# Other banks for the layer projections at two norms of the first block, and another place for one norm's spread

## The reference

```python
def first_block(x, ...):                                   # one layer
    z = rmsnorm(h, norm_mix_pre) @ w_in                    # pool input, q, k, v, gates
    y_pool = pool_mixer(p) @ w_branch_pool
    y_attn = moba_attention(q, k, v) @ w_branch_attn
    m = sigmoid(g_pool) * y_pool + sigmoid(g_attn) * y_attn
    h = h + rmsnorm(m @ w_out, norm_mix_post)              # joint 1: norm, residual, next norm
    u2 = rmsnorm(h, norm_mlp_pre)
    a = square(relu(u2 @ w_up))                            # 1024 -> 4096
    h = h + rmsnorm(a @ w_down, norm_mlp_post)             # joint 2: the same
def second_block(x, p, ...):                               # two layers: diff. attention, windowed attention
    hn = rms_norm(h, attn_norm[i]); h = h + mixer(hn)
    h = h + conv_ffn(rms_norm(h, ffn_norm[i]))
    gate = sigmoid(rms_norm(h, ple_norm[i]) @ ple_w_gate[i])
    h = h + (p[i] @ ple_w_proj[i]) * gate                  # p @ ple_w_proj depends on no h
    return rms_norm(h, final_norm)
```

## Time and profile before

| | |
|---|---|
| median of 3 runs | 1990.87 us (1989.4 to 1992.05) |
| profiled execution | 1990.34 us, its span 1988.6 us |
| mean granted TensorE clock | 0.994 of full speed |
| TensorE busy | 1951.0 us (98%) |
| VectorE, ScalarE, GpSimd busy | 1195.8, 924.6, 1113.9 us |
| joint 1 (columns to the next product) | 319.78 to 333.28 us |
| joint 2 | 688.47 to 701.28 us |

### The profile page before, as it was taken

How to read it: one execution, slowest core, us unless ns; L and a number is a source line. 1 busy time by engine, 2 the same in 40 slices (tenths; PEclk the granted TensorE clock), 3 DMA queues, 4 the chain that set the end, 5 groups by cost and what they waited for, 6 DMA issues and landing times.

```text
span 1988.6 us, 25389 instructions
## 1 busy us (share of the span) xinstructions
PE 1951.0 (98%) x9308; PEld 1602.0 (81%) x9308; DVE 1195.8 (60%) x2004; ACT 924.6 (46%) x1740; POOL 1113.9 (56%) x847
## 2 busy tenths in 40 slices
PE   8999999999999999999999999999999999999997
PEld 6877887888888877878788888888777888888886
DVE  6773324353433488877676646856688775745855
ACT  5653336433333356545353433445477543443443
POOL 5344545454444456454566665755784576666652
PEclk9999999999999999999999999999999999999998
DMA  4122233232232321111323222223110322222221
GB/s 159 64 70 95 96 106 128 85 111 101 96 113 91 122 82 64 53 59 59 128 95 105 96 97 95 96 89 109 64 54 33 128 96 105 96 85 98 103 96 53
DMA packets 52107, 182.73 MB, mean 92 GB/s; under 512 B 5776, under 2 KB 6160, under 8 KB 51984
## 3 DMA queue, kind: packets, MB, share of 16 engines
q1 hardware_dynamic: 51984, 181.12, 26.0%
HBM read 174.80 MB, written 6.29 MB: 91 GB/s over the span
## 4 chain that ended last, share of the span: by engine, by line
PE 95%; DVE 3%; ACT 1%; issue 0%; DMA 0%; POOL 0%; SPq 0%; DVEq 0%; POOLq 0%
PE b L394 29%; PE b L396 28%; PE b L395 28%; PE b L416 3%; PE b L408 2%; PE b L449 1%; PE b L459 1%; PE b L440 1%; PE b L409 1%; PE b L439 1%; PE b L410 1%; PE b L427 0%; PE b L429 0%; PE b L428 0%; DMA raw<-in_w_first 0%
## 5 line engine op out<-in xcount | busy, mean ns | idle before, releaser
L240 POOL TENSOR_TENSOR ra<-raw,ra 128x512 fp32r<-128x512 f32 x632 | 881.0, 1401 | 781.7 <-ACT ra L284 779.1
L394 PE MATMUL b<-ra 128*128 128x512 f32 x2528 | 1001.9, 396 | 20.3 <-POOL ra L240 9.6
L396 PE MATMUL b<-ra 128*128 128x512 f32 x2528 | 986.6, 390 | 0.0
L395 PE MATMUL b<-ra 128*128 128x512 f32 x2528 | 985.8, 390 | 0.0
L284 ACT ACTIVATE ra<-raw 128x512 fp32r<-128x512 f32 x632 | 392.6, 628 | 536.4 <-PE b L396 529.9
L394 PEld LDWEIGHTS b<-ra 128*128 128x128 f32 x2528 | 475.8, 188 | 126.6 <-issue 17.1
L396 PEld LDWEIGHTS b<-ra 128*128 128x128 f32 x2528 | 475.4, 188 | 101.2
L395 PEld LDWEIGHTS b<-ra 128*128 128x128 f32 x2528 | 476.1, 188 | 93.2
L732 DVE TENSOR_TENSOR h<-b,h 128x512 f32<-128x512 f32 x136 | 91.7, 683 | 60.3 <-PE b L396 59.6
L623 DVE TENSOR_TENSOR tmp<-b,rb 128x512 f32<-128x512 f32 x64 | 43.9, 690 | 126.2 <-PE b L396 126.1
L616 DVE TENSOR_TENSOR ra<-b,ra 128x512 fp32r<-128x512 f32 (+4 forms) x166 | 91.7, 567 | 18.1 <-ACT ra L335 15.4
(11 more groups left out here) (277 smaller groups left out, 1929.8 us busy)
## 6 DMA issues: line engine op xcount, KB each, us to landing
raw<-in_f_g SPq DMA_DIRECT2D x40, 512.0 KB, 3.5
raw<-in_f_v SPq DMA_DIRECT2D x40, 512.0 KB, 3.5
raw<-in_f_d SPq DMA_DIRECT2D x40, 512.0 KB, 3.4
raw<-in_w_up SPq DMA_DIRECT2D x32, 512.0 KB, 3.5
raw<-in_w_down SPq DMA_DIRECT2D x32, 512.0 KB, 3.5
raw<-in_p_g SPq DMA_DIRECT2D x16, 512.0 KB, 3.5
raw<-in_w_gp SPq DMA_DIRECT2D x8, 512.0 KB, 3.5
raw<-in_w_ga SPq DMA_DIRECT2D x8, 512.0 KB, 3.5
```

What stands on the lines that cost most here:

```text
L240: e.tensor_tensor(wl, src, wh.bitcast(F), ALU.subtract).then_inc(*w_low.mark(n))
L394: e.matmul(ps, wh[:, c:c + 128], xh, start=start, stop=False)
L395: e.matmul(ps, wh[:, c:c + 128], xl, start=False, stop=False)
L396: last = e.matmul(ps, wl[:, c:c + 128], xh, start=False, stop=stop)
```

## The change

`LATER` gets a fifth value, -0.4, for rank -6, and the spread of a norm with `keep` gets this rank: it may be placed up to 0.4 us before its inputs are estimated ready, where it was placed 0.6 us after. The banks of both joints are dealt anew. At joint 1 `LB7` stands as 5, 6, 0, 1, 2, 3, 4: `spare` is now 2 and 3, and the projection takes 0, 4, 1 in turn. At joint 2 `spare` is 4 and 5, and the projection takes 2, 6, 3 in turn.

```diff
-LATER = (1.5, 4.0, 0.6, 2.5)
+LATER = (1.5, 4.0, 0.6, 2.5, -0.4)
...
-        yield -4 if x["rank"] == -2 else -3, "pe", lambda: None if bank_free[STB] is None else (v, *bank_free[STB])
+        yield -6 if x["keep"] else -4 if x["rank"] == -2 else -3, "pe", lambda: None if bank_free[STB] is None else (
+            v, *bank_free[STB])
         x["spread"] = t = spread(0, v)
...
-        spare += LB7[4:]
-        yield from layer_projection(0, LB7[:4])
+
+
+        spare += LB7[4:6]
+        yield from layer_projection(0, [LB7[2], LB7[6], LB7[3]])
...
-                yn3, u3 = post_norm("mlp_post", ("attn", 0), now("pe"), [4, 5, 6])
+                yn3, u3 = post_norm("mlp_post", ("attn", 0), now("pe"), [4, 5])
...
-        yield from layer_projection(1, [0, 1, 2, 3])
+        yield from layer_projection(1, [2, 6, 3])
```

## The result

The changed kernel takes 1987.85 us (median of 20 runs, 1985.84 to 1989.36) against 1992.16 us of the kernel before in 20 runs beside it: ratio 0.9979, 95% interval 0.9973 to 0.9985, so 4.2 us less (3.0 to 5.4). On a second chip the median was 1986.23 against 1991.42 us: 0.9974 (0.9964 to 0.9985). The profiled execution took 1987.47 us, its span 1985.7, where 1990.34 and 1988.6 stood before: 2.9 us less.

A forecast was written before the change was run, and what follows sets the result against it. TensorE, busy 98% of the span, bounds the kernel; both joints wait for ScalarE's copy. Gains of 1.2 + 1.6 + 0.2 = 3.0 us take the median from 1990.87 to 1987.9 us, range 1985.0 to 1991.5.

The forecast's parts named there:

- joint 1: The step from the first block's attention to its MLP; 2.57 us of TensorE time lost there before the change.
- joint 2: The step from the MLP to the second block's attention; TensorE idle 2.40 us there before the change.
- The spread, 1.2 us sooner: At joint 1, the spread behind 12 matmuls after the columns instead of 18, starting about 324.5 instead of 325.70.
- Seven steps in 3.61 us: At joint 1, ScalarE's awaited copy still seven steps, 3.61 us, behind the new chunk's high part, so starting at 331.09.
- TensorE's start, 0.99 us behind the copy's: At joint 1, the next layer's first product starts 0.99 us after ScalarE's awaited copy starts, at 332.08: 1.20 us gained.
- The low clock behind joint 1, 1.6 us: The 1.2 GHz stretch after joint 1 stays away once the wait shrinks from 2.4 to 1.1 us: 1.6 us gained.
- The wait for line 702, 1.1 us: At joint 2, the first projection waits for VectorE's accumulation on bank 2: 1.1 us later, between 0.9 and 1.3.
- Joint 2's end, 0.2 us gained: The product ending joint 2 starts at 701.03 instead of 701.28; 0.2 us taken, between -0.3 and 0.6.
- A (the low clock stays): Rival: the low-clock stretch does not go, or returns at another wait; gain 1.4 us, 1989.5 us; chance 0.20.
- B (both waits vanish): Rival: ScalarE's queue does not decide, and both joints' waits vanish; gain 5.6 us, 1985.3 us; chance 0.13.
- Rival C: Bank 2's wait at joint 2 is not regained, lower clock there, joint 1 keeps its own; +1.5, 1992.4 us; chance 0.10.
- D (all shifts cancel): Rival: at both joints the spread or second projection waits, so the change does nothing; 1990.9 us; chance 0.07.

## Why the prediction was right, and where it was off

The forecast of 1987.9 us, by 1.2 + 1.6 + 0.2 = 3.0 us, came in at 1987.85 and inside its range; against the runs of before beside it the gain is 4.2 us. The profiled execution gave 2.9 us, of which the segments of the joints are 3.16 and the start 0.26 of loss. That the time itself came so close is in part luck: the forecast started from the median of three runs, 1990.87, and twenty runs of the same kernel gave 1992.16, 1.3 us more. The gain, 3.0 us by the forecast, is at the lower end of the measured interval (3.0 to 5.4).

- **Bank 4 at joint 1, 0.1 us.** Right: 318.67 to 318.99 is 0.32 us instead of 0.23.
- **The spread, 1.2 us sooner.** Right: less the 0.26 us by which joint 1 starts later it stands at 324.46; forecast "about 324.5". VectorE's root ended at 324.50 + 0.16 = 324.66, 0.06 us before it.
- **Seven steps in 3.61 us.** Right to the hundredth, and with it that "not needed next" does not shorten ScalarE's queue. The high part and the copy stand at 327.54 and 331.15, forecast 327.48 and 331.09.
- **TensorE's start, 0.99 us behind the copy's.** Wrong by 0.3 us: it is 0.69 (332.10 for 331.41), since fewer waits stand before the matmul. I had taken a distance of the trace for a constant; in it lie 0.36 us from the copy's end, of which 0.3 go with the waits, as the test with fewer waits shows. So joint 1 gained 1.44 us and not 1.20.
- **The low clock behind joint 1, 1.6 us.** Right in size: 3.06 - 1.44 = 1.62. The prediction called it "the least certain term" because joint 2 had no drop. In five executions with over 2 us of idle at joint 1 the stretch came five times, in the nine others never, the one with dummy matmuls among them. The Trainium skill (TensorE: Matmul & The Clock Gate, Terms) prices such a stretch at its length times the share withheld; the trace agrees, with 1.62 us for the prediction's estimate of 1.7.
- **The wait for line 702, 1.1 us.** Right: the start is at 683.21 where 682.27 was due (685.07 less the 2.80 us that all is sooner), 0.94, and the columns at 688.88 by the old count of time, forecast 688.89; the spread at 693.45, forecast 693.44.
- **Joint 2's end, 0.2 us gained.** Mis-sized at the place, near in the end: the product starts 0.45 us sooner (698.03 + 2.80 = 700.83 for 701.28), again by the shorter way from the copy to the matmul. The copy itself stood at 700.15 by the old count, 0.12 us later than forecast: the prediction took joint 1's 2.98 us from the spread to the first high part, where the rows of joint 2 give 2.80 before, and the new profile has 3.08. Of the 0.45 us, 0.3 is given back in the second block before the last line 427, in both profiles of the change. Nearly all of it goes at one place on TensorE:

```profile
826.91 0.63 PE L416 MATMUL b<-ident,fa 128*128 128x128 f32 x4 [0.19 <-DVE fa L581]
```

The matmuls ahead of this one start 3.14 us sooner than before, this one 2.89. The wait stands in both profiles of the change (0.19 and 0.17 us) and at this place in none of before or of the version with bank 3 first, whose segment keeps its gain. What makes VectorE late there is not shown.
- **What the forecast did not contain.** The kernel before pays the low stretch at joint 2 too, in some executions: over all versions, in one of six with an idle of 1.87 us or more there. The change's idles of 0.78 and 0.75 us had none in two. A pair of profiles need not show this part of the gain in the median. It fits that joint 1 alone was timed at -2.4 and the whole change at -4.2 and -5.2, with joint 2's segment worth only 0.1; but these intervals overlap, and one execution is no rate. How much of the 4.2 us it makes stays open.

Of the rivals, A (the low clock stays) fell with the window behind joint 1. B (both waits vanish) fell for the change, but is nearly what the banks alone do: my objection, that ScalarE's queue decides, held only for the order that the sooner spread makes. Rival C had the wait of bank 2 right and what follows from it wrong: joint 2 got its time back, no lower clock came there, and joint 1's went. The awaited copy at joint 2 stood at 697.35, which is 700.15 by the old count, before the 700.9 from which it decides. The Trainium skill's rule that small idle pieces on cycling banks bring the lower clock (TensorE: Matmul & The Clock Gate, A second HAM failure mode: psum-queue depth-cycling), on which C leaned, did not show: two idles, of 0.78 and 0.75 us within 15 us, left the clock at 1.00. D (all shifts cancel) fell with the spread and the new order of the banks, which moved as forecast.

The deeper miss is in the reading of the change, not in its sum. I priced the sooner spread as the source of the 1.2 us at joint 1. The segments say the opposite: alone it gives 0.26 there, and on top of the banks it costs 0.29 there, which its 0.39 at joint 2 about makes up. What counts is which tile's copy the next product awaits and how many of ScalarE's steps stand between; an earlier spread lets new chunks in front of that copy.

## What to carry to other kernels

When a wait ends on a shared in-order queue, count the steps between what starts the queue and the awaited one, and ask whether making the start earlier also puts other work in front. Compare versions by segments between instructions that stand at the same place in both, since single executions start and throttle differently. Where an instruction waits for several values of one semaphore, ask for the highest first, so that the others can be left out.

## What the runs showed of the hardware

- Waits on one semaphore that have already been met are not free: from the end of ScalarE's copy to TensorE's matmul it is 0.36 us where three waits for earlier copies stand ahead of the awaited one, and 0.06 us where they are left out.
- An idle of 2.1 to 2.4 us of TensorE was followed by a stretch at 1.2 GHz at joint 1 in five of five executions, at joint 2 (1.87 to 2.4 us) in one of six, which cost 1.6 and 1.7 us; behind idles of up to 1.1 us at the joints it never came. What differs between the joints was not found.
- A low stretch behind the 1.6 us wait for line 616, near 1531 us, came in ten of fourteen executions and was worth 1.4 us where its absence can be told from the rest (1035.66 for 1037.10). It is in no term of the change, and moved single profiles by as much as the change's own smaller parts.
